# The last 22 gate tiles of an input projection as 11 pairs by seven block products, the block inversion interleaved with their sums, chunk 1 of the scan loaded later

## The reference

```python
u = x @ w_in                        # 1024 x 7688, columns of A, B, C and of the gates
# A: gated delta rule, chunk-causal (64 tokens); B: RWKV-7; C: window attention
lower = where(strict, einsum(k_beta, k) * decay, 0)
t_inv = triangular_solve(lower + eye, eye)      # per chunk and head
mix = sum over branches of sigmoid(gate) * (branch @ w_branch)
x = LayerNorm(alpha * x + mix @ w_out)
x = LayerNorm(alpha * x + (silu(x @ ffn_gate) * (x @ ffn_up)) @ ffn_down)
```

## Time and profile before

| | us |
|---|---|
| median of 3 runs | 1816.58 (1815.66 to 1818.18) |
| span of the profiled execution | 1816.2 |
| PE busy | 1781.5 (98%) |
| DVE busy | 1141.4 (63%) |
| ACT busy | 665.2 (37%) |
| POOL busy | 584.6 (32%) |

### The profile page before, as it was taken

The page is one execution under the profiler, slowest core; times in us unless marked ns, Lnnn a source line. Parts: engine busy times, 40 slices in busy tenths (PEclk is TensorE's granted clock), DMA queues, the critical chain, the costliest instruction groups (busy, mean ns, idle before and its releaser), DMA issues. The chain is left out here.

```text
span 1816.2 us, 28096 instructions
## 1 busy us (share of the span) xinstructions
PE 1781.5 (98%) x11148; PEld 1471.3 (81%) x11148; DVE 1141.4 (63%) x1354; ACT 665.2 (37%) x1126; POOL 584.6 (32%) x418
## 2 busy tenths in 40 slices
PE   8999999999999999999999999999999999999997
PEld 7778787777788888788878788888888888888886
DVE  2856665666419930377768854966666665665577
ACT  3534434244421211355542231343333333344341
POOL 1211222212213332344415452755455554500000
PEclk9999999999999999999999999999999999999999
DMA  6255575235673377377665573225545455488464
GB/s 178 50 112 140 141 180 138 65 76 155 166 206 93 93 162 228 126 237 245 186 211 173 163 236 97 101 70 183 171 133 171 143 175 179 139 286 300 169 226 155
DMA packets 386434, 293.24 MB, mean 161 GB/s; under 512 B 172428, under 2 KB 318412, under 8 KB 384256
## 3 DMA queue, kind: packets, MB, share of 16 engines
q1 hardware_dynamic: 310080, 237.63, 44.1%
q10 hardware_dynamic: 76224, 53.81, 10.3%
HBM read 196.33 MB, written 94.98 MB: 160 GB/s over the span
## 5 line engine op out<-in xcount | busy, mean ns | idle before, releaser
L168 PE MATMUL bank<-xhi,w_hi 128*128 128x512 f32 x960 | 379.0, 395 | 2.5 <-ACT turned L847 1.7
L170 PE MATMUL bank<-xhi,w_lo 128*128 128x512 f32 x960 | 374.4, 390 | 0.0
L169 PE MATMUL bank<-xlo,w_hi 128*128 128x512 f32 x960 | 373.8, 389 | 0.0
L472 POOL TENSOR_TENSOR w_lo<-w_raw,w_hi 128x1024 fp32r<-128x1024 f32 x59 | 168.3, 2853 | 538.1 <-ACT w_hi L854 538.1
L168 PEld LDWEIGHTS bank<-xhi,w_hi 128*128 128x128 f32 x960 | 180.3, 188 | 43.3 <-issue 6.8
L170 PEld LDWEIGHTS bank<-xhi,w_lo 128*128 128x128 f32 x960 | 180.2, 188 | 38.4
L169 PEld LDWEIGHTS bank<-xlo,w_hi 128*128 128x128 f32 x960 | 180.4, 188 | 36.1
L2044 POOL TENSOR_TENSOR ff_ring_lo<-ff_w_sums,ff_ring_hi 128x512 fp32r<-128x512 f32 x88 | 125.7, 1430 | 74.6 <-ACT ff_ring_hi L2326 74.4
L2044 POOL TENSOR_TENSOR ff_ring_lo<-ff_raw,ff_ring_hi 128x512 fp32r<-128x512 f32 x66 | 96.2, 1460 | 149.4 <-ACT ff_ring_hi L2326 149.4
L834 ACT ACTIVATE work<-bank 128x512 f32<-128x512 f32 x68 | 40.7, 598 | 244.7 <-PE bank L170 228.4
L175 PE MATMUL b_ps<-x1hi,ff_ring_hi 128*128 128x512 f32 x264 | 102.9, 390 | 0.0
(11 more groups left out here) (418 smaller groups left out, 3968.7 us busy)
## 6 DMA issues: line engine op xcount, KB each, us to landing
w_raw<-in_w_in ACTq DMA_DIRECT2D x61, 512.0 KB, 4.3
hid_ops<-y SPq DMA_DIRECT2D x77, 256.0 KB, 2.8
ff_raw<-hid_ops SPq DMA_DIRECT2D x77, 256.0 KB, 3.9
op<-opnd SPq DMA_DIRECT2D x16, 1152.0 KB, 5.5
u<-work ACTq DMA_DIRECT2D x68, 256.0 KB, 4.3
b_gate<-u SPq DMA_DIRECT2D x24, 512.0 KB, 3.6
ff_raw<-in_ffn_gate SPq DMA_DIRECT2D x22, 512.0 KB, 4.5
ff_raw<-in_ffn_up SPq DMA_DIRECT2D x22, 512.0 KB, 5.7
```

The costliest lines, as they stand in the source:

```text
L168: pe.matmul(out, w_hi, x_hi, start=first, stop=False)
L169: pe.matmul(out, w_hi, x_lo, start=False, stop=False)
L170: return pe.matmul(out, w_lo, x_hi, start=False, stop=last)
L472: pool.tensor_tensor(w_lo[b][:, :, :], w_raw[b][:, :, :], as_f32(w_hi[b][:, :, :]), ALU.subtract).then_inc(w_lo_done, 1)
```

## The change

The last 22 tiles of the order, all of gates, leave `ITEMS` and become 11 pairs. A pair is two tiles by two halves of the tokens, and two halves of the inner dimension: a product of 2x2 blocks, made by seven block products of 12 matmuls each instead of eight (96 matmuls become 84). `seven_products` gives their order `SEQ` of (product, pair), 77 in all. The input's sums (z parts: `x12`, `z5`, `z6`, `z7`, `z4`, their high and low parts) are made once by VectorE and ScalarE. Four sums of weights a pair are made by VectorE (`weight_sum`; those of pair 0 by POOL, `first_sums`). ScalarE loads pairs, makes high parts, copies partial results out of PSUM (`snap`), applies the sigmoid once VectorE has added the rest (`settle`, then `close`) and stores (`store_result`).

VectorE's inversion stands no longer behind the preparation alone: from product 12 on its instructions are placed between sums and settlings, by a running credit `room`. The tile U_SV comes earlier, with its own buffer, and the turns of the values come behind those of the RWKV heads. Turns that would fall behind half tile 77 (`LATE`, two of them) come behind products 0 and 1. SP loads chunk 0 in the block as before, chunk 1 behind product 7 of the last pair without waiting for its landing, and chunk 2 in the scan. The last settling and the last sigmoid go into the scan's block (`last_sum`, `last_half`). Buffers are laid over one another anew, and the program's scratch area for DMA rings is made smaller. Cut to its core:

```diff
-    fillers = [*range(U_SQ, U_SV), *range(U_Z, A_TILES), U_SV, *range(U_GATE, U_GATE + 24)]
+    fillers = [U_SQ, U_SV, *range(U_SQ + 1, U_SV), *range(U_Z, A_TILES), *range(U_GATE, U_GATE + 24)]
...
+    PAIRS = [(ORDER[NR + 2 * f], ORDER[NR + 2 * f + 1]) for f in range(NPAIRS)]
+    ORDER = ORDER[:NR]
+    NT_IN = NR
...
+        turn_after[max(q for q in turn_after if turn_after[q][0] == "rwkv") + 1 + g] = ("value", g)
...
+    LATE = [turn_after[q] for q in sorted(turn_after) if q >= NQ]
+    ITEMS += LATE
...
+    SEQ, AT = seven_products(NPAIRS)
+    RING = 4
+    slot_of = lambda i: (i + 2) % RING
...
+        INV_STEPS, INV_FROM = 2 + 2 * (NB - 1), 12
...
+            def low_part(i):
+                p, f = SEQ[i]
+                src = pair_raw[f % 2][:, raw_block[p], :] if p in raw_block else part_sum[p]
+                pool.wait_ge(w_hi_done, NT_IN + i + 1)
+                pool.tensor_tensor(lo_pair[:, slot_of(i), :], src, as_f32(hi_pair[:, slot_of(i), :]), ALU.subtract).then_inc(w_lo_done, 1)
+
+            def first_sums():
+                a11, a12, a21, a22 = (pair_raw[0][:, n, :] for n in range(4))
+                pool.wait_ge(outs, 4)
+                pool.tensor_tensor(part_sum[7], a11, a21, ALU.subtract).then_inc(first_sum, 1)
+                pool.tensor_tensor(part_sum[5], a21, a22, ALU.add).then_inc(first_sum, 1)
+                pool.wait_ge(first_sum, 2)
+                pool.wait_ge(low_done, 4)
+                pool.tensor_tensor(part_sum[6], part_sum[5], a11, ALU.subtract).then_inc(first_sum, 1)
+                yield
+                pool.wait_ge(first_sum, 3)
+                pool.wait_ge(turn_stored[0], 16 * turn_count[0])
+                pool.tensor_tensor(part_sum[3], a12, part_sum[6], ALU.subtract).then_inc(first_sum, 1)
+                yield
+            first = first_sums()
+            for i in range(len(SEQ)):
+                if i in (2, 4):
+                    next(first)
+                low_part(i)
...
-            for c in range(DEEP):
-                load_chunk(sp, c, early, opnd, xinv, early_landed, early_inv)
-                sp.wait_ge(early_landed, 112 * c + 112)
-                sp.wait_ge(early_inv, 48 * c + 48)
+            load_chunk(sp, 0, early, opnd, xinv, early_landed, early_inv)
+            sp.wait_ge(early_landed, 112)
+            sp.wait_ge(early_inv, 48)
             sp.wait_ge(cols_landed, 16 * 17)
+            sp.wait_ge(mm_p, AT[7, NPAIRS - 1] + 1)
+            load_chunk(sp, 1, early, opnd, xinv, early_landed, early_inv)
...
+            def product(i):
+                p, f = SEQ[i]
+                pe.wait_ge(w_lo_done, NT_IN + i + 1)
...
+                for k in range(4):
+                    cols_ = slice(k * P, (k + 1) * P)
+                    last = more_dot(pe, to, hi_pair[:, slot_of(i), cols_], lo_pair[:, slot_of(i), cols_], hi[:, k, :], lo[:, k, :], p in (1, 2, 7) and k == 0)
+                last.then_inc(mm_p, 1)
+            for i in range(len(SEQ)):
+                product(i)
+                if i < len(LATE):
+                    turn_tokens(LATE[i])
...
+            for j in range(len(SEQ)):
+                p, f = SEQ[j]
+                if p in (1, 6, 5, 3):
+                    snap(j)
+                if j and SEQ[j - 1][0] in (2, 5, 4):
+                    close(j - 1)
+                if j + RING < len(SEQ):
+                    high_part(j + RING)
+                if j == 0:
+                    for item in LATE:
+                        finish(item)
+                if j in (1, 3):
+                    high_sum({1: 7, 3: 4}[j])
+                if p == 3:
+                    store_result(12, f, (snapped, SNAP_AT[3, f]))
+                if j and SEQ[j - 1][0] in (2, 5, 4):
+                    store_result(*closes[-1], (closed, len(closes)))
+                if j + 3 < len(SEQ) and SEQ[j + 3][0] == 4 and SEQ[j + 3][1] + 2 < NPAIRS:
+                    load_pair(SEQ[j + 3][1] + 2)
...
+            def z_part(out, a, b, op, n):
+                if n:
+                    dve.wait_ge(z_step, n)
+                dve.tensor_tensor(out, a, b, op).then_inc(z_step, 1)
+            whole_block = lambda k, h: (as_f32(block_of(xhi, k, h)), as_f32(block_of(xlo, k, h)))
+            dve.wait_ge(mm_done, done_at["value", 1])
+            z_part(x12, *whole_block(0, 1), ALU.add, 0)
+            z_part(z5, *whole_block(0, 0), ALU.add, 0)
+            z_part(z5, x12, z5, ALU.subtract, 2)
             mask_gdn(2)
             scale(3)
             mask_gdn(3)
+            dve.wait_ge(silu_done, 12)
+            z_part(z7, *whole_block(1, 1), ALU.add, 0)
+            dve.wait_ge(g_stored[0], 96)
+            dve.wait_ge(mm_done, turned_by("gdn", 2, "k"))
+            z_part(z6, z7, z5, ALU.subtract, 4)
+            z_part(z7, z7, x12, ALU.subtract, 5)
+            z_part(z4, *whole_block(1, 0), ALU.add, 0)
+            z_part(z4, z4, z6, ALU.subtract, 7)
+
+            def low_sum(p):
+                dve.wait_ge(z_hi, (6, 5, 7, 4).index(p) + 1)
+                if p == 7:
+                    dve.wait_ge(g_stored[1], 96)
+                dve.tensor_tensor(ops[p][1], {6: z6, 5: z5, 7: z7, 4: z4}[p], as_f32(ops[p][0]), ALU.subtract).then_inc(z_lo, 1)
+            low_sum(6)
...
+            def weight_sum(f, p):
+                a11, a12, a21, a22 = (pair_raw[f % 2][:, n, :] for n in range(4))
...
+                dve.tensor_tensor(out, a, b, op).then_inc(w_sum, 1)
+
+            def settle(j):
+                p, f = SEQ[j]
...
+                dve.wait_ge(mm_p, j + 1)
+                dve.wait_ge(snapped, SNAP_AT[before, f])
+                dve.tensor_tensor(result_of(to, f), result_of(to, f), src, ALU.add).then_inc(added, 1)
...
+            def invert():
+
+                parts = [steps(part) for part in PARTS]
+                for done in range(INV_STEPS):
+                    i = (done + 1) // 2
+                    for k in range(2):
+                        if done:
+                            dve.wait_ge(inv_step[k], done)
+                        next(parts[k]).then_inc(inv_step[k], 1)
+                        yield 0.07 + (PARTS[k].stop - PARTS[k].start) * i * i * (0.0019 if done % 2 else 0.00115)
+            inversion, room = invert(), 0.0
+            for j in range(len(SEQ)):
+                p, f = SEQ[j]
+                work_now = 0
+                if p in (2, 5, 4) and j < len(SEQ) - 1:
+                    settle(j)
+                    work_now += 1
+                todo_now = {2: [(7, 1)], 3: [(5, 1)], 4: [(6, 1)], 6: [(3, 1)]}.get(j, [])
+                g = f - (p in (1, 2))
+                if 1 <= g < NPAIRS - 1:
+                    todo_now = todo_now + [(one, f + (p == 6)) for one in {6: (7, 5), 1: (6,), 2: (3,)}.get(p, ())]
+                for one, pair in todo_now:
+                    weight_sum(pair, one)
+                    work_now += 1
...
+                if j == INV_FROM:
+                    dve.wait_ge(inv_landed, 32 * R)
+                if j >= INV_FROM:
+                    room += 2.5 - 0.7 * work_now
+                    while room > 0:
+                        took = next(inversion, None)
+                        if took is None:
+                            break
+                        room -= took
+            for _ in inversion:
+                pass
...
+                dve.tensor_tensor(out, out, y_bank(NPAIRS - 1), ALU.add).then_inc(added, 1)
...
+                if c == 1:
+                    sp.wait_ge(loaded[0], 224)
+                    sp.sem_inc(landed[1], 112)
+                    sp.wait_ge(loaded[1], 96)
+                    sp.sem_inc(inv_landed[1], 48)
+                if c == 2:
+                    sp.wait_ge(*last_stored)
                     load_chunk(sp, c, tiles, opnd, xinv, landed[b], inv_landed[b])
```

More of the change, by code:

```diff
@@ new lines, in project_and_prepare @@
+        halves = [slice(h * HALF, (h + 1) * HALF) for h in range(2)]
+        block_of = lambda x, k, h: x[:, 4 * k:4 * k + 4, halves[h]]
+        ops = {1: (block_of(xhi, 0, 0), block_of(xlo, 0, 0)), 2: (block_of(xhi, 1, 0), block_of(xlo, 1, 0)),
+               3: (block_of(xhi, 1, 1), block_of(xlo, 1, 1)), 4: (block_of(xhi, 0, 1), block_of(xlo, 0, 1)),
+               5: (t5h[:, :, :], t5l[:, :, :]), 6: (t6h[:, :, :], t6l[:, :, :]), 7: (t7h[:, :, :], t7l[:, :, :])}
+        of_slabs = lambda first: work[:, first:first + 2, :].rearrange("p r (k n) -> p (r k) n", n=HALF)
@@ new lines, in project_and_prepare @@
+        turned_words = turned_tile[1][:, :, :].rearrange("p n d -> p (n d)")
+        apart = {(11, 1): result[12], (21, 1): turned_words, (21, NPAIRS - 1): turned_words}
+        result_of = lambda c, f: apart.get((c, f), result[c])
+        raw_block = {1: 0, 2: 1, 4: 3}
+        pair_at = lambda f: (w_landed[f % 2], 16 * ((NT_IN + 1 - f % 2) // 2) + 32 * (f // 2 + 1))
+        x_bank = lambda f: z_ps[:, f % 2, :]
+        y_bank = lambda f: bank[1][:, :] if f == NPAIRS - 1 else a_ps[:, f % 2, :]
@@ L1192, in _ @@
```

(11 more changed lines are left out.)

217 lines of the change are left out of this document (169 added, 48 removed).

## The result

| | us |
|---|---|
| before, median beside the changed kernel | 1817.38 |
| after, median | 1839.82 (1838.28 to 1841.03) |
| ratio | 1.0126, interval 1.0113 to 1.0139 |
| span of the profiled execution | 1837.4, before 1816.2 |

The change makes the kernel slower by 22 us; 11.6 were forecast. The direction and the mechanism were right; three terms were too small, the start of the pairs by the most. Products are counted from 0 here, as in the prediction.

A forecast was written before the change was run, and what follows sets the result against it. The projection was taken to be bound by TensorE's queue. Terms -29.9 + 2 + 27 + 10 + 2.5 = +11.6 on 1816.2 gave span 1827.8, forecast 1828 us; forecast case 1821 to 1838 (chance 0.53), wider range 1811 to 1843.

The forecast's parts named there:

- What is removed, -29.9: Last 22 dense tiles: 1056 matmuls become 924, 132 fewer at 0.2267 us each, saving 29.9 us.
- The start at 508.9: Half tile 78's place: two turns of values move ahead of it, so it starts at 508.9 us, not 507.85.
- Start of the pairs, +2 (0 to 5): First products: pair 0's fourth sum of weights comes late for product 4, costing 2 us (0 to 5).
- the free VectorE: Start of the pairs: input sums take some 2.4 us each, six ready at about 511.3, before product 4 at 521.
- The lock, +10 (0 to 20): In the pairs, VectorE's multiplications and POOL's subtractions exclude each other, moving the inversion's end by 10 us (0 to 20).
- Rival A: VectorE keeps pace in the pairs: the +10 and +2.5 terms go to 0 to 3; +1, 1818 us; chance 0.2.
- rival B: The lock decides: VectorE and POOL need 22 us a pair, 25 us over the stretch; +30, 1847 us; chance 0.14.
- extreme of 25.7 us a pair: If POOL ran beside nothing of VectorE, not even reductions: 25.7 us a pair, inversion's end moved by 57 us.
- The inversion ends 11.6 us before the last matmul: VectorE's written order puts the inversion's last instruction behind product 71's settling, 11.6 us before TensorE's end, formerly 95.6.
- The chain, 39 - 11.6 = +27: Behind the inversion: stores 24, chunk 0 9, chunk 1's issues 6, 39 us less 11.6 covered; +27 us (24 to 34).
- Start of the scan, +2.5 (0 to 6): Scan's start: late load of the attention's quarter and lower clock after TensorE's idling cost 2.5 us (0 to 6).
- ScalarE's stores at 0: Storing quadrant 21's result takes 5.2 us against two products' 5.4: covered at the median, 0 to 5 inside the 10.

The follow-up runs named there:

- without an inversion: Changed kernel without the inversion's 128 instructions (inverse all zeros), their end signalled at product 12: 1802.96 us, ratio 0.9926.
- the late signal: Changed kernel without the inversion's instructions, their end signalled at product 72, where the inversion ends in the changed kernel: 1826.37 us, ratio 1.0054.
- the one with direct waits: Changed kernel with TensorE and POOL waiting for chunk 1 on its loads' own semaphores, not on SP's passed-on ones: 1836.87 us, ratio 1.0105.
- the one with chunk 1 in the scan: Changed kernel with chunk 1's nine loads issued inside the scan, at its first chunk, not in front of it: 1845.90 us, ratio 1.0153.

## Why the prediction was right and wrong

- **What is removed, -29.9: right.** 132 matmuls fewer; without an inversion nothing else bounds the stretch behind the start, the last matmul starts at 727.69 and the time falls below before.
- **The start at 508.9: 510.23.** 1.3 us late, from a lower granted clock near 280 us, in a stretch that the change doesn't touch (last section).
- **Start of the pairs, +2 (0 to 5): measured 6, wrong.** The step that failed is the free VectorE: it took the z parts at 2.4 us, and named pair 0's fourth sum as what comes late. What came late was POOL's low part for product 2, as POOL made its first sums at 3.3 us, in turn with the z parts. The prediction knew the lock, and costed it only for the inversion. This is the largest miss; with 2 in place of 6 the time would have lain inside the stated range.
- **The lock, +10 (0 to 20): right, 9.7.** The 77 products took from 510.23 to 739.37 = 229.1 us, the prediction had 731.3 - 508.9 = 222.4; the start explains 4 of the 6.7. The other 2.7 are not the lock's: the 68 products from 8 to 76 take 187.6 us without an inversion and not 68 x 2.72 = 185.0, a term that the prediction put at nothing (0.8 of it is one wait for ScalarE near the end). The lock's 9.7 stand on top and go when POOL's subtractions are halved. Rival A (VectorE keeps pace) falls with these 9.7, and so does rival B at 25 us. The price of a sum of weights in the feed-forward was a good guide, 1.23 us on the mean: here 32 sums from 560 to 728 take 1.24 on the mean, 0.94 to 1.65 by group.

 On the lock the Trainium skill, "SBUF — State Buffer", in "Summary: rules for kernel authors", says that the one that issues second fully blocks until the other has finished. The rows at the start of the pairs agree within 0.3 us: 2.29 and 1.28 us in turn are 3.57, and either takes 3.3. The prediction's extreme of 25.7 us a pair, in which not even the reductions run beside POOL, did not occur: the slowest stretch, products 20 to 50, has 91.5 us for 30 products, 21.4 a pair.
- **The inversion ends 11.6 us before the last matmul: right**, 739.37 - 728.25 = 11.1; the written order decides it.
- **The chain, 39 - 11.6 = +27: right**, 37.7 and a pause of 26.6 us; the late signal alone costs 23.4. It is the largest term of the loss.
- **Start of the scan, +2.5 (0 to 6): measured 4.8** (behind the first matmul of the scan the span has 1071.4 us, 1066.6 before). The step was mis-attributed: idle and clock, which it names, are 0.8 us. The relay of the landing through SP's queue was not seen; the prediction said of this edit only that chunk 2 has time, and chunk 2 has none left once the relay is gone (2.0 us of TensorE). 3.8 of the 4.8 us lie in the first two chunks; of the last 1.0 the cause stays open.
- **ScalarE's stores at 0: not seen as a cost.** The stalls in the middle (six of 0.6 to 1.7 us from 579 to 658, ended by VectorE's settling, ScalarE's copies and POOL) go with the inversion.

Sum of the misses: 1.3 (clock near 280 us) + 4 (start of the pairs) + 2.7 (products) - 0.8 (pause 26.6 for 27.4) + 2.3 (start of the scan) = 9.5, against 1837.4 - 1827.8 = 9.6.

## What to carry to other kernels

Work moved from a free stretch into one where another engine excludes it costs its own time, the other's, and everything that hangs on its end: count this for every pair of neighbours, in the set-up phase too. Where a long chain of stores and loads follows the moved work, keep matmuls behind it, or leave it where it was. A landing that a third queue passes on is as late as that queue: let the users wait on the load's own semaphore, and look whether the next load is in time for it, or the gain goes there.

## What the runs showed of the hardware

The kernels differ between executions in a place that no edit touches. Near 277 us TensorE waits for a turned tile that ScalarE has to copy; the rows are those of the kernel before, the changed one, the one with direct waits and the one with chunk 1 in the scan:

```profile
279.65 0.47 PE L168 MATMUL bank<-xhi,w_hi 128*128 128x512 f32 x1 [1.73 <-ACT turned L847]
```
```profile
279.66 0.47 PE L168 MATMUL bank<-xhi,w_hi 128*128 128x512 f32 x1 [2.11 <-ACT turned L951]
```
```profile
277.52 0.47 PE L168 MATMUL bank<-xhi,w_hi 128*128 128x512 f32 x1 [0.61 <-ACT turned L951]
```
```profile
281.01 0.76 PE L168 MATMUL bank<-xhi,w_hi 128*128 128x512 f32 x1 [3.15 <-ACT turned L949]
```

In the stretch behind it (280 to 290 us) the granted clock is 1.00 in the first and the third, and 0.83 in the second and the fourth, a third of 10 us at 1.2 GHz, 1.7 us by that:

```profile
280.00:290.00 10.00, 10.00 (x40) 8.11 (x39) 0.33 (x1) 4.06 (x7) 2.39 (x1) 0.83 0.58 145
```

From the end of this wait to product 0 it is 230.6 us in the changed kernel and 229.0 in the one with direct waits: the clock is worth 1.6 us. With the wait the start of product 0 spreads from 506.5 to 511.6 us over the profiled executions of the kernels with eleven pairs. That is a part of the spread of single times, which is 2 to 11 us in a series (before too: up to 9), and a reason why one profiled span says little about 2 us. What ScalarE's copy waits for there was not followed. A pause of 28 us, on the other hand, costs less behind itself (0.8 us, ahead of the scan's small matmuls) than one of 2.7 us at the start of the pairs (matmuls at half speed, 1.6 us).
